# The last feed-forward block cut into groups of 4, 6, 6 and 6 chunks instead of 6, 8 and 8

## The chip, the cores and the metric

The kernel runs on one core of a Trainium2 chip. TensorE (PE) multiplies matrices, VectorE (DVE), ScalarE (ACT) and GpSimd (POOL) work elementwise, and transfers are issued from the queues of SyncE (SP), ScalarE and GpSimd. The metric is the device time of one execution in microseconds (us), as the median of several runs. Before the change it is 2786.47 us (3 runs, 2783.3 to 2787.67).

## The reference

Two trunk layers run over 512 latent tokens and 256 context tokens of width 1024. Each layer is half a SwiGLU feed-forward block, a mixer, and another half feed-forward block, so there are four feed-forward blocks, numbered f = 0 to 3 in the kernel. The last block, f = 3, runs over the 512 latent tokens alone, since the context is not part of the output.

```python
def swiglu(h, w1, w3, w2):
    return (jax.nn.silu(h @ w1) * (h @ w3)) @ w2

def _half_ffn(h, g, m, k, w1, w3, w2):
    y = swiglu(_modulate(h, g, m, k), w1, w3, w2)
    return h + (0.5 * m[:, :, 3 * k + 2] * y).astype(h.dtype)
```

`w1` and `w3` are 1024 x 2816, `w2` is 2816 x 1024. All arrays are float32.

## The kernel before, in words

Features lie on the 128 partitions and tokens on the free axis. The 2816 hidden features are 22 chunks of 128. A chunk needs two up products, one with `w1` (the gate) and one with `w3`; the two together are called a pair. A feed-forward block is cut into groups of chunks (`GROUPS`, L56). For each group the kernel first makes the hidden chunks (the pairs) and then one down pass: for each of the 8 output chunks j it multiplies the group's hidden chunks by their part of `w2` in PSUM and adds the result to the residual `x` (L2210). So each group costs one pass of 8 additions to `x`, and the matmuls of all the down passes together do not depend on the grouping.

Every float32 matrix product is made of three matmuls, because each operand is split into a rounded high part and the rest: weights times `hi`, weights times `lo`, and the weights' rest times `hi`. ACT makes the high part of a weight tile (L1362, L1427), DVE the rest by a subtraction (L2014, L2086). Weight tiles land in two buffers, `raw0` and `raw1`; the next transfer into a buffer starts when DVE has made the rest of the tile before (L569).

There are two kinds of pairs. A plain pair (first group of each block, `g == 0`) is 2 x 8 x 3 = 48 matmuls over all tokens, 512 columns each in the last block. A pair of seven products (all other groups; function `seven_products`, L791) splits both the weights and the tokens in halves and makes a 2 x 2 block product from seven products instead of eight (a Strassen-Winograd form): 7 x 4 x 3 = 84 matmuls over half of the tokens, 256 columns each in the last block. It needs sums of weight blocks. These are made ahead of time by accumulating transfers that GpSimd issues (`weight_sums`, L2902), in units of up to three pairs: seven transfers in four dependent steps, from HBM to HBM. A pair loads four tiles: two of sums into `raw` (L599), and `a11` and `a2` straight from the weights (L582, L588). It also needs sums of the tokens, made once for each block from the normalised activations: `sums(f, k)` for k = 0 to 3 on DVE (six instructions, L2062 to L2067), then `sum_hi` on ACT (L1399) and `sums_lo` on DVE (L2073). In a first group of six chunks all four are made behind the plain pairs 2 to 5. In a first group of four chunks, as in blocks 0 to 2, k = 0 and 1 are made behind pairs 2 and 3, and k = 2 and 3 in the down pass, at j = 1 and 3 (L1572, L2351, L2353).

The engines work their own programs in order and meet at semaphores. Around the change these orders matter. On ACT in a down pass, the high part of the tile for j + 2 comes first and then what `also(j)` holds. On DVE in a down pass, it is the addition to `x` of output j, then the rest of the tile for j + 2, then `also(j)`. In a pair of seven products, DVE makes the rests of `S1` and `A11` of the next pair before that of `A12` of this pair:

```python
                if not last:
                    weight_lo(f, g, i + 1, "S1")
                    weight_lo(f, g, i + 1, "A11")
                weight_lo(f, g, i, "A12")
```

The sixth product of pair i (on `A12`, L822) therefore waits for the sums of pair i + 1 to have landed. On GpSimd's queue the order is by hand (from L2978): the sums of the squares for a norm (`add_squares`) and the weight sums of the groups take turns. The sums of group 1 of the last block stand ahead of `add_squares(4)`, those of group 2 behind `add_squares(5)`, which ends just as the last block's first matmuls start.

Of the kernel before, what the change touches and what calls it, by code (L numbers as in the profile page):

```python
# [52 lines left out]


AB_IN_T, AB_OUT_T, CD_IN_T, CD_OUT_T = 24, 8, 20, 8
GROUPS = ((4, 6, 6, 6),) * 3 + ((6, 8, 8),)  # L56
HC = 6
BASE = {}
_t = 0
for _name, _n in (("ffn0", 2 * FC + KC * len(GROUPS[0])), ("ab_in", AB_IN_T), ("ab_out", AB_OUT_T),  # L60
                  ("ffn1", 2 * FC + KC * len(GROUPS[1])), ("ffn2", 2 * FC + KC * len(GROUPS[2])),
# [6 lines left out]
def first_chunk(f, g):  # L68
    return sum(GROUPS[f][:g])

# [12 lines left out]

NSEVEN = FC - GROUPS[0][0]

# [122 lines left out]
def build(nc, dr):  # L208
    ctx = ExitStack()
    with ctx:  # L210
# [1137 lines left out]
        def _(act):  # L1348
# [192 lines left out]
            def ffn(f, look, n_sq, ns, ns_sq):  # L1541
                n = NORM_OF[f]
                for g, size in enumerate(GROUPS[f]):
                    b, d, last = up_tile(f, g), down_tile(f, g), g == len(GROUPS[f]) - 1
                    for i in range(size):
                        ch, nk = first_chunk(f, g) + i, size if i == size - 1 else KC
                        if seven(f, g):
                            seven_act(f, g, i)
                            continue
                        if f and ch == 0:  # L1550
                            act.wait_ge(u_gate, 2 * LATE_UP.index(n) + 2)
                            act.activation(hidden_bufs(f)[0][:, 0, 0:ns], hfu[:, 0:ns], ACT.Copy).then_inc(h_hi, 1)
                            if f < 3:
                                act.wait_ge(h_ready, f * FC + 1)
                                load_scb(scb)
                                for q in range(2):
                                    load_mod(MODS[f][0] + q, mraw)
                            continue
                        plain_pair(f, ch, i, b + 2 * i, nk, ns)
                        if f == 0 and ch == 0:  # L1560
                            act.wait_ge(xn_ready, 8)
                            for q in range(2):
                                load_mod(q, mraw)
                        if 0 < f < 3 and ch == 1:
                            take_scb(f + 2, scb)
                        next_mods(f, ("up", ch))
                        if ch >= 2:
                            sum_hi(f, ch - 2)

                    def also(j):  # L1570

                        if f < 3 and g == 0 and j in (1, 3):  # L1572
                            sum_hi(f, 2 + j // 2)
                        if g == 0 and j == 5:
                            first_sum_hi(f)
                        if not last and j >= KC - 2:
                            for name in (("A11",), ("S1", "S2"))[j - KC + 2]:
                                weight_hi(f, g + 1, 0, name)
                        if j and not last:
                            next_mods(f, ("down", g, j - 1))  # L1580
                        if (f, g, j) == (2, 2, 3):
                            act.wait_ge(dl_set, 1)
                            act.activation(coef[:, 1, :], coef[:, 0, :], ACT.Exp, scale=-1.0).then_inc(coef_exp, 1)
                            act.wait_ge(dl_set, 3)
                            act.activation(dl[:, 2:4], dl[:, 0:2], ACT.Exp).then_inc(coef_exp, 1)

                    if last:
                        down(d, look, size, n_sq, ns_sq, also)
                    else:
                        down(d, 0, size, None, ns, also)  # L1590
# [411 lines left out]
        def _(dve):  # L2002
# [311 lines left out]
            def ffn(f, look, segs, nn=None):  # L2314
                n, ns = NORM_OF[f], segs[-1][1]
                for g, size in enumerate(GROUPS[f]):
                    b, d, last = up_tile(f, g), down_tile(f, g), g == len(GROUPS[f]) - 1
                    for i in range(size):
                        ch, nk = first_chunk(f, g) + i, size if i == size - 1 else KC

                        def ahead():
                            if f == 0 and ch < 2:
                                gate_dots(2 * ch)
                            if f < 3:
                                dot_mods(f, ("up", ch))

                        def behind():
                            if f == 0 and ch < 2:
                                gate_dots(2 * ch + 1)
                            if ch >= 2:  # L2330
                                sums(f, ch - 2)
                                sums_lo(f, ch - 2)

                        if seven(f, g):
                            seven_dve(f, g, i)
                        elif f and ch == 0:
                            bh, bl = hidden_bufs(f)
                            dve.wait_ge(h_hi, plain_chunk(f, 0) + 1)
                            dve.tensor_tensor(bl[:, 0, 0:ns], hfu[:, 0:ns], bh[:, 0, 0:ns].bitcast(F32), ALU.subtract
                                              ).then_inc(h_ready, 1)  # L2340
                        else:
                            plain_pair(f, ch, i, b + 2 * i, nk, ns, ahead, behind)
                    if f == 1 and g == 0:
                        late_gate(2)
                    if last and nn is not None:
                        prep(nn)

                    def also(j):

                        if g == 0:  # L2350
                            if f < 3 and j in (1, 3):  # L2351
                                sums(f, 2 + j // 2)
                            if f < 3 and j in (2, 4):  # L2353
                                sums_lo(f, 1 + j // 2)
                            if j == 5:
                                first_sum_lo(f)
                        if not last and j == KC - 2:
                            for name in ("A11", "S1", "S2"):
                                weight_lo(f, g + 1, 0, name)
                        if (f, g, j) == (2, 2, 2):  # L2360
                            cd_consts()
                        if (f, g, j) == (2, 2, 5):
                            cd_coefs()
                        if last or j < KC - 1:
                            dot_mods(f, ("down", g, j))

                    if last:
                        down(d, look, size, n, segs, nn, also)
                    else:
                        down(d, 0, size, n, segs, None, also)  # L2370
# [520 lines left out]
        def _(pool):  # L2891
# [10 lines left out]
            def weight_sums(f, g):  # L2902

                r, row = SEVEN_ROUNDS.index((f, g)), 2 * (f * FC + first_chunk(f, g))
                for i, n in sum_units(f, g):
                    base = 16 * SUM_DMAS * SUM_AT_UNIT[f, g, i]
                    tile = dr["w13"][row + 2 * i:row + 2 * (i + n)].rearrange("(i q) p c -> q p i c", q=2)
                    to = dr["sums"][r][:, i:i + n]
                    S = [to[:, :, q, :] for q in range(4)]
                    pool.wait_ge(sum_landed, base)  # L2910
                    pool.dma_start(S[0], tile[1][:, :, 0:512]).then_inc(sum_landed, 16)
                    pool.dma_start(S[1], tile[0][:, :, 0:512]).then_inc(sum_landed, 16)
                    pool.dma_start(to[:, :, 2:4, :].rearrange("p i b c -> p i (b c)"), tile[0]).then_inc(sum_landed, 16)
                    pool.wait_ge(sum_landed, base + 16 * 3)
                    pool.dma_start(S[0], tile[1][:, :, 512:D], accum_op=ALU.add).then_inc(sum_landed, 16)
                    pool.dma_start(S[2], tile[1][:, :, 0:512], accum_op=ALU.add).then_inc(sum_landed, 16)
                    pool.wait_ge(sum_landed, base + 16 * 5)
                    pool.dma_start(S[1], S[0], accum_op=ALU.add).then_inc(sum_landed, 16)
                    pool.wait_ge(sum_landed, base + 16 * 6)
                    pool.dma_start(S[3], S[1], accum_op=ALU.add).then_inc(sum_landed, 16)  # L2920
# [71 lines left out]
            add_squares(4, T)  # L2992
            cd_pool()
            add_squares(5, NLAT)
            weight_sums(3, 2)


def host_arrays(a):
# [110 lines left out]
```

## Time and profile before

| | us |
|---|---|
| median of 3 runs | 2786.47 |
| the profiled execution | 2784.83 |
| its span, first to last instruction | 2783.1 |
| TensorE busy | 2675.1 (96%) |
| VectorE busy | 2056.2 (74%) |
| ScalarE busy | 1176.3 (42%) |
| GpSimd busy | 390.2 (14%) |
| the last block's first down pass starts | 2486.9 |
| TensorE's last matmul ends | 2779.9 |

TensorE's busy share counts the modelled time of matmuls that overlap, so it says that the engine is rarely idle, and not at which rate it works. For the rate one takes a stretch without gaps and divides it by the number of matmuls in it. Times within the execution are counted from the span's start. "Landing" is the time from the issue of a transfer to its end. In the names of operands a buffer's number is left out: `a` is `a11` or `a2`, `wh` and `wl` are the high parts and rests of `raw`.

### The profile page before, as it was taken

The numbers are of one execution on the slowest core, as the hardware profiler recorded it, in microseconds if no ns is written. First come the engines' busy times: TensorE is split into PE (matmuls) and PEld (weight loads), VectorE is DVE, ScalarE is ACT, GpSimd is POOL, SyncE is SP. The second block draws the span as 40 slices with busy tenths as digits, with TensorE's granted clock in tenths as the row PEclk, the third lists the DMA queues.
The fourth block names the chain that finished last, engine by engine and source line by source line (L and its number), as shares of the span: only waits on it lengthen the run. The fifth ranks groups of instructions, "written<-read, shape, count | busy, mean of one in ns | idle before, by whom it ended". The sixth has DMA issues, their size and how long they took to land.

```text
span 2783.1 us, 40131 instructions
## 1 busy us (share of the span) xinstructions
PE 2675.1 (96%) x15624; PEld 2512.6 (90%) x15624; DVE 2056.2 (74%) x3184; ACT 1176.3 (42%) x1860; POOL 390.2 (14%) x312
## 2 busy tenths in 40 slices
PE   5999999999988999999999999999999989999999
PEld 5999999998976899999999999999997775788898
DVE  7887878774558587878777877787878667666674
ACT  3233333346447644332323523242436866533342
POOL 3111111110012521111111211100022410211000
PEclk8999999999999999999999999999999999999999
DMA  9888989621120047889897589874522110378453
GB/s 347 209 228 248 274 252 267 169 67 54 59 62 1 1 143 203 245 224 281 229 274 212 137 221 258 248 214 131 165 69 83 61 46 1 114 201 235 145 165 125
DMA packets 161691, 464.13 MB, mean 167 GB/s; under 512 B 13281, under 2 KB 14433, under 8 KB 160609
## 3 DMA queue, kind: packets, MB, share of 16 engines
q1 hardware_dynamic: 87200, 247.65, 26.3%
q0 software_dynamic: 56448, 146.81, 24.3%
q10 hardware_dynamic: 17856, 67.12, 6.8%
q8 instruction: 125, 2.05, 0.3%
q14 instruction: 62, 0.50, 0.0%
HBM read 459.43 MB, written 148.90 MB: 219 GB/s over the span
## 4 chain that ended last, share of the span: by engine, by line
PE 78%; DVE 11%; DMA 5%; ACT 3%; issue 3%; POOL 0%; ACTq 0%; SPq 0%; DVEq 0%; POOLq 0%
PE banks L698 11%; PE banks L702 11%; PE banks L700 11%; PE banks L786 9%; PE banks L788 9%; PE banks L787 9%; DMA raw<-sums 4%; PE banks L705 3%; PE banks L709 3%; PE banks L707 3%; DVE banks L2019 1%; DVE tmp L2292 1%; PE banks L1233 1%; DVE wl L2086 1%; DVE wl L2014 1%
## 5 line engine op out<-in xcount | busy, mean ns | idle before, releaser
L1362 ACT ACTIVATE wh<-raw 128x1024 fp32r<-128x1024 f32 (+2 forms) x194 | 181.8, 937 | 611.8 <-PE banks L702 458.7
L2019 DVE SCALAR_TENSOR_TENSOR banks<-mraw,scb 128x1024 f32<-128x1024 f32 x240 | 304.9, 1270 | 11.6 <-DMA mraw<-in_wmn 7.9
L2014 DVE TENSOR_TENSOR wl<-raw,wh 128x1024 fp32r<-128x1024 f32 (+2 forms) x216 | 234.3, 1085 | 95.5 <-ACT wh L1362 93.2
L1427 ACT ACTIVATE wh<-raw 128x512 fp32r<-128x512 f32 (+1 forms) x210 | 161.6, 774 | 326.6 <-DMA raw<-sums 156.7
L698 PE MATMUL banks<-hh,wh 128*128 128x384 f32 x1056 | 270.4, 337 | 9.3 <-DVE wl L2014 9.0
L786 PE MATMUL banks<-xh,wh 128*128 128x384 f32 (+1 forms) x796 | 258.0, 324 | 12.8 <-DVE wl L2086 12.7
L702 PE MATMUL banks<-hh,wl 128*128 128x384 f32 x1056 | 269.9, 336 | 0.0
L700 PE MATMUL banks<-hl,wh 128*128 128x384 f32 x1056 | 269.7, 336 | 0.0
L788 PE MATMUL banks<-xh,wl 128*128 128x384 f32 (+1 forms) x796 | 256.6, 322 | 0.0
L787 PE MATMUL banks<-xl,wh 128*128 128x384 f32 (+1 forms) x796 | 256.5, 322 | 0.0
L698 PE MATMUL banks<-xh,wh 128*128 128x384 f32 x880 | 230.7, 343 | 21.4 <-DVE xl L2284 12.0
L700 PE MATMUL banks<-xl,wh 128*128 128x384 f32 x880 | 225.2, 336 | 0.0
L702 PE MATMUL banks<-xh,wl 128*128 128x384 f32 x880 | 224.9, 336 | 0.0
L2086 DVE TENSOR_TENSOR wl<-raw,wh 128x512 fp32r<-128x512 f32 (+1 forms) x210 | 180.9, 866 | 43.6 <-ACT wh L1427 43.5
L698 PEld LDWEIGHTS banks<-hh,wh 128*128 128x128 f32 x1056 | 191.5, 189 | 11.5 <-DVE wl L2014 11.2
L702 PEld LDWEIGHTS banks<-hh,wl 128*128 128x128 f32 x1056 | 192.3, 189 | 0.0
L700 PEld LDWEIGHTS banks<-hl,wh 128*128 128x128 f32 x1056 | 192.2, 189 | 0.0
L698 PEld LDWEIGHTS banks<-xh,wh 128*128 128x128 f32 x880 | 158.4, 189 | 29.9 <-issue 16.0
L786 PE MATMUL banks<-th,wh 128*128 128x384 f32 (+1 forms) x560 | 180.5, 322 | 0.0
L787 PE MATMUL banks<-tl,wh 128*128 128x384 f32 (+1 forms) x560 | 180.5, 322 | 0.0
L788 PE MATMUL banks<-th,wl 128*128 128x384 f32 (+1 forms) x560 | 180.5, 322 | 0.0
L786 PEld LDWEIGHTS banks<-xh,wh 128*128 128x128 f32 x796 | 150.0, 188 | 16.3 <-DVE wl L2086 16.3
(427 smaller groups left out, 6225.5 us busy)
## 6 DMA issues: line engine op xcount, KB each, us to landing
raw<-sums SPq DMA_DIRECT2D x140, 512.0 KB, 6.0
sums<-in_w POOLq DMA_DIRECT2D x88, 768.0 KB, 8.5
mraw<-in_wmn ACTq DMA_DIRECT2D x120, 512.0 KB, 5.7
a<-in_w SPq DMA_DIRECT2D x70, 512.0 KB, 4.3
sums<-in_w POOLq DMA_DIRECT2D x22, 1536.0 KB, 8.8
sums<-sums POOLq DMA_DIRECT2D x44, 768.0 KB, 9.6
raw<-in_w SPq DMA_DIRECT2D x80, 384.0 KB, 4.3
raw<-in_w SPq DMA_DIRECT2D x52, 512.0 KB, 3.9
```

The costliest lines, as they stand in the source:

```text
L698: pe.matmul(bank(h), W, tokens(rh, h), start=(k == 0), stop=False)
L700: pe.matmul(bank(h), W, tokens(rl, h), start=False, stop=False)
L702: mm = pe.matmul(bank(h), L, tokens(rh, h), start=False, stop=(k == nk - 1))
L705: pe.matmul(G[slot][:, a:b], W, rh[:, k, a:b], start=(k == 0), stop=False)
L786: pe.matmul(thirds(bank), W, rh(k), start=(k == 0), stop=False)
L787: pe.matmul(thirds(bank), W, rl(k), start=False, stop=False)
L788: mm = pe.matmul(thirds(bank), L, rh(k), start=False, stop=(k == 3))
L1362: act.activation(wh[slot][:, 0:nk * P], raw[slot][:, 0:nk * P], ACT.Copy).then_inc(hi_done, 1)
L1427: act.activation(W_HI[slot_of(name, last)], W_SRC[name], ACT.Copy).then_inc(w_hi, 1)
L2014: dve.tensor_tensor(wl[slot][:, 0:nk * P], raw[slot][:, 0:nk * P], wh[slot][:, 0:nk * P].bitcast(F32), ALU.subtract).then_inc(lo_done, 1)
L2019: return dve.scalar_tensor_tensor(B67[:], tile, 1.0, scv[:, s, :], ALU.mult, ALU.mult, accum_out=out)
L2086: dve.tensor_tensor(W_LO[to], W_SRC[name], W_HI[to].bitcast(F32), ALU.subtract).then_inc(w_lo, 1)
```

## The change

`GROUPS[3]` becomes (4, 6, 6, 6), the same as for the other three blocks. All functions that go by `GROUPS` follow: the first group has four plain pairs (six before), the three others have 18 pairs of seven products (16 before), and there are four down passes of 4, 6, 6 and 6 chunks (three of 6, 8 and 8 before). Two of the four token sums move from the plain pairs into the first down pass, on ACT and on DVE. GpSimd makes weight sums for 6 pairs ahead of `add_squares(4)` (8 before) and for 12 pairs behind `add_squares(5)` (8 before).

```diff
-GROUPS = ((4, 6, 6, 6),) * 3 + ((6, 8, 8),)
+GROUPS = ((4, 6, 6, 6),) * 4
...
-                        if f < 3 and g == 0 and j in (1, 3):
+                        if g == 0 and j in (1, 3):
                             sum_hi(f, 2 + j // 2)
...
-                            if f < 3 and j in (1, 3):
+                            if j in (1, 3):
                                 sums(f, 2 + j // 2)
-                            if f < 3 and j in (2, 4):
+                            if j in (2, 4):
                                 sums_lo(f, 1 + j // 2)
...
-            weight_sums(3, 2)
+            for g in (2, 3):
+                weight_sums(3, g)
```

## Rows read from the trace of the kernel before

**Rows 1.** The page's first part: the span and TensorE's busy time.
```profile
span 2783.1 us, 40131 instructions
PE 2675.1 (96%) x15624; PEld 2512.6 (90%) x15624; DVE 2056.2 (74%) x3184; ACT 1176.3 (42%) x1860; POOL 390.2 (14%) x312
```

**Rows 2.** Busy times by stage, last block: stretch, length, engines (instructions), clock, transfers' share.
```profile
2465.10:2486.87 21.77, 21.77 (x97) 18.02 (x96) 14.67 (x22) 7.51 (x10) 2.25 (x3) 1.00 0.70 199
2486.87:2521.56 34.69, 33.24 (x145) 26.83 (x144) 18.62 (x26) 9.72 (x13) 4.68 (x4) 1.00 0.89 234
2521.56:2612.15 90.59, 83.21 (x674) 82.19 (x673) 65.91 (x111) 42.47 (x79) 6.99 (x8) 0.98 0.73 209
2612.15:2655.69 43.54, 43.54 (x194) 36.04 (x193) 17.29 (x20) 8.89 (x11) 0.00 (x0) 1.00 0.40 125
2655.69:2736.15 80.46, 80.46 (x673) 80.45 (x672) 64.75 (x109) 42.82 (x78) 0.00 (x0) 1.00 0.55 168
2736.15:2779.25 43.10, 43.10 (x193) 35.67 (x191) 15.50 (x17) 7.23 (x8) 0.00 (x0) 1.00 0.34 113
```

**Rows 3.** Waits of 2521 to 2612: who for whom, total us, times, longest.
```profile
ACT wh L1427 <- DMA raw<-sums: 20.9, 9, 5.6
...
PE banks L786 <- DVE wl L2086: 7.4, 5, 3.0
```

**Rows 4.** TensorE's timeline, second group, pairs 0, 1, 3: start, duration, instruction, idle before.
```profile
2531.87 0.38 PE L786 MATMUL banks<-xh,wh 128*128 128x256 f32 x1 [2.97 <-DVE wl L2086]
...
2533.59 0.42 PE L787 MATMUL banks<-tl,weh 128*128 128x256 f32 x1
...
2536.80 0.29 PE L787 MATMUL banks<-xl,wah 128*128 128x256 f32 x1
...
2543.88 0.39 PE L786 MATMUL banks<-xh,wh 128*128 128x256 f32 x1 [0.23 <-DVE wl L2086]
...
2567.31 0.39 PE L786 MATMUL banks<-xh,wh 128*128 128x256 f32 x1 [1.62 <-DVE wl L2086]
```

**Rows 5.** The chain that ended last, in the same pair: start, duration, what.
```profile
2522.47 6.76 DMA raw<-sums
...
2531.13 0.69 DVE wl L2086
```

**Rows 6.** GpSimd's timeline: starts of the last block's sum units, their last transfer, an earlier idle time.
```profile
2045.60 1.40 POOL L2896 COPY ssq<-sq 128x768 f32<-128x768 f32 x1 [206.06 <-ACT sq L1479]
...
2415.95 0.79 POOL L2911 DMA_DIRECT2D sums<-in_w  x1
...
2529.39 0.73 POOL L2911 DMA_DIRECT2D sums<-in_w  x1 [7.58 <-DMA sums<-sums]
...
2566.23 1.14 POOL L2920 DMA_DIRECT2D sums<-sums  x1 [7.29 <-DMA sums<-sums]
```

**Rows 7.** Issues, KB, median us to landing: 2490 to 2521, 2580 to 2736, whole span.
```profile
raw<-in_w SPq DMA_DIRECT2D x4, 384.0 KB, 6.1
...
raw<-sums SPq DMA_DIRECT2D x20, 512.0 KB, 3.6
...
raw<-in_w SPq DMA_DIRECT2D x24, 256.0 KB, 4.9
```

**Rows 8.** Timelines of VectorE and ScalarE at the first down pass's start.
```profile
2489.49 0.68 DVE L2062 TENSOR_TENSOR tmp<-xh,xl 128x512 f32<-128x512 f32 x1
...
2492.53 0.85 ACT L1399 ACTIVATE th<-tf 128x768 fp32r<-128x768 f32 x1 [4.02 <-DVE tf L2067]
...
2494.28 0.75 DVE L2210 SCALAR_TENSOR_TENSOR x<-banks,modG,x 128x512 f32<-128x512 f32 x1
2494.94 0.95 DVE L2014 TENSOR_TENSOR wl<-raw,wh 128x768 fp32r<-128x768 f32 x1
```

**Rows 9.** Block 2's first down pass (4 chunks, 768 tokens): as a stage, and TensorE's wait.
```profile
1633.80:1672.30 38.50, 35.56 (x194) 34.80 (x194) 33.83 (x55) 11.49 (x15) 4.94 (x4) 0.96 0.85 216
...
PE banks L698 <- DVE wl L2014: 2.9, 1, 2.9
```

## What the change should do to the time

> **What bounds the kernel now.** I read the page's first part first: TensorE is busy for 2675 of 2783 us [rows 1], so the time is TensorE's work plus its gaps. Then the stages of the last block [rows 2], which the change alone touches. In order they are two of the plain pairs, the first down pass (6 chunks), eight pairs of seven products, a down pass (8), eight more pairs, and the last down pass (8). The two halves do the same kind of work and don't take the same time: eight pairs take 90.6 us in the second group and 80.5 us in the third. Without gaps a 512-column matmul takes 43.54 / 192 = 0.227 us and a 256-column one 80.46 / 672 = 0.1197 us. At these rates the first down pass should take 144 x 0.227 = 32.7 us; it took 34.7, so it lost 2.0, and the second group lost 90.59 - 80.46 = 10.1.
>
> What differs is GpSimd. While it moves weight sums (from 2415.95 to the last transfer issued at 2566.23, landed near 2574 [rows 6]) the transfer engines are busy for 0.73 to 0.89 of the time, and for 0.34 to 0.55 after it [rows 2]. The waits name the link: ScalarE waits 20.9 us for tiles of sums to land, and TensorE 7.4 us, in five gaps, for a weight's rest [rows 3]. The chain shows one such gap [rows 5]: the tile lands 6.76 us after its issue, and ScalarE and VectorE need 2.6 us more until the rest for the sixth product begins (L2086 at 2531.13), because VectorE has the next pair's two rests ahead of it. In the third group a tile of sums lands in 3.6 us [rows 7], and TensorE has no gap. So the last block is bound by TensorE when GpSimd moves nothing, and by the landing of weights when it does.
>
> The first gap is 2.97 us. After it the matmuls start 0.12 us apart, and from 2533.4 to 2536.8 0.213 us apart: 15 matmuls at the 1.2 GHz level [rows 4], 15 x 0.093 = 1.4 us more. The granted clock of the stage is 0.98 where the others have 1.00 [rows 2]. The four shorter gaps of that group, 0.23 to 1.62 us [rows 4], have no such stretch behind them.
>
> **The change part by part.** Sums are against the profiled execution (2784.83 us, span 2783.1); the median is 1.64 us above it, and I add the same difference to the median.
>
> 1. TensorE's work. Two plain pairs go, 21.8 us, and two pairs of seven products come, 2 x 80.46 / 8 = 20.1 us [rows 2]. The down matmuls stay 22 x 8 x 3 = 528. Sum: -1.65 us. This is all that the change can gain by itself.
> The Trainium skill ("TensorE: Matmul & The Clock Gate", section "Wait — 56ns, not 53.3ns?") has a matmul of N columns start every N / 2.4 GHz + 2.5 ns. By that a plain pair is 10.4 us and a pair of seven 9.2 us, and the two would save 2.4 us. The trace is 5 to 10% slower at both widths and decides.
>
> 2. The first down pass with 4 chunks. I count from its start, D, to the sixth product of the next pair. Now this is 2531.87 - 2486.87 = 45.0 us, of which TensorE works 32.7 + 60 x 0.12 = 39.9: lost 5.1. With 4 chunks it works 21.8 + 7.2 = 29.0. What else must happen in this time is the order of VectorE and ScalarE: the last token sum of the plain pairs stands ahead of the tile for j = 2. With 6 chunks VectorE works on it from 2489.49, ScalarE makes its high part at 2492.53, and only then come the addition to x and the rest of the tile (2494.94 to 2495.9, D + 9.0) [rows 8], when the first two outputs took 8.2 us. With 4 chunks the tiles are a third narrower, so this comes at about D + 8.4, and TensorE is through with its two outputs at D + 5.9: a gap of 2.5 us. Block 2 has this pass at 768 tokens and shows that gap: 2.9 us, granted clock 0.96, 38.5 us for 192 x 0.173 = 33.3 us of matmuls, lost 5.2 [rows 9]. With 512 tokens the matmuls give a third less cover and VectorE's work does not shrink as much. Then two token sums follow at j = 1 and 3, of some 3.0 us on VectorE each (2489.49 to 2492.5 [rows 8]), with the tiles for j = 4 and 6 behind them on both engines: rests done at about D + 14.6 and D + 22. The narrow tile's landing of 4.9 us [rows 7] fits in beside this. The sums for the next pair are issued at D + 22, land 7 us later (6.76 in rows 5), and their second rest is ready 1.8 us after that, at D + 30.8; from there to the sixth product it is 9.4 us, as now (2522.45 to 2531.87). Together 40.2, lost 11.2, so +6.1 us. Bounds: as much lost as in block 2 and the 3.0 us gap of the pair after it, 8.2, so +3.1; or the tiles come at 9.2 us for two throughout, as they did in the present pass (ScalarE at 2502.21 and 2511.38), so lost 16, +11. I take +6.1, since the orders are those of the code.
>
> 3. The rest of the second group. From the sixth product on it lost 80.28 - 73.3 = 7.0 us (four gaps, and the stretch at 1.2 GHz). The group is now six pairs, of which the last has no next pair to wait for; the stalls were in pairs 0 to 4, and these remain. 0, with 1 us either way.
>
> 4. GpSimd's queue. It now moves 12 pairs of sums from 2416 on, in four units of three. A unit took (2529.39 - 2415.95) / 2 = 56.7 us [rows 6], so it ends at about 2643 and not at 2574. That is 69 us more under traffic. Nobody waits for the sums as such: the third unit lands near 2586, the last group starts near 2699. Ahead of `add_squares(4)` one unit of two pairs falls away; GpSimd idles for 206 us there [rows 6], TensorE has no gap then, so 0.
>
> 5. The second down pass, now 6 chunks under traffic. The tiles of 384 KB land in 6.1 us [rows 7]; with 0.85 + 0.96 us for the two halves the cycle of two tiles is 8.0 to 9.2 us against TensorE's 8.2, and it starts with two tiles in hand. +0.3, between 0 and +2.
>
> 6. The third group, first pair. Now it follows a pass of 6 chunks under traffic as the second group's did. The second rest would be ready about when the down pass ends, the sixth product 9.4 us later, TensorE's work before it 7.2: a gap of 2.2 us, and perhaps the slow stretch. I take +3.2, between 0 and 4.4 (3.0 + 1.4, what the second group paid).
>
> 7. Pairs 1 to 3 of the third group, from about 2610 to the end of the traffic. Without the first pair the second group lost 10.1 - 4.4 = 5.7 us in four pairs, 1.4 each (the gap and the restart): +4.2 us, between 0.7 (the smallest gap three times) and 6.5 (the largest four times).
>
> Sum: -1.65 + 6.1 + 0 + 0 + 0.3 + 3.2 + 4.2 = +12.15 us. Span 2795.3, execution 2797.0, median 2798.6 us. The lower ends give +1, the upper ones +24; they would not all meet.
>
> **The rivals.**
> Small: the traffic is spread thinner. In its last 69 us tiles land soon enough, and parts 5 to 7 give 1.5 us, with part 2 near its low end: +3 us, 2789.5. For it: the second pair's gap was only 0.23 us. Against it: the landing is what the five gaps of rows 3 have in common.
> Large: the first pass runs at 9.2 us for two tiles, the second pass loses 2 us, and the third group's stalls are as large as the largest: +20 us, 2806. For it: the present pass had this cycle twice.
> Clock: the Trainium skill (same page, section "HAM oscillation — how this bites in real kernels") tells of kernels in which each wait for a transfer puts TensorE back to half rate. Here that would be the 1.4 us stretch behind each of the about eight gaps that remain or come, in place of one or two: +8 us on the forecast, 2807. Only the gap of 2.97 us has such a stretch [rows 3, 4]; I give it little.
> Faster: the stalls of the second group depend on how a tile's landing meets the transfers of the sums. The group starts some 25 us earlier, in another unit. Were the tiles to land there within 7.2 - 2.6 = 4.6 us, the point from which it decides, its 10.1 us would go, and with a first pass at its low bound and nothing in the third group the sum is -1.65 - 10.1 + 3.1 = -8.6 us, 2778. Against it: all of the traffic's rows in this block lie above that point (6.1 and 6.76 us), and no unit differs from the others.
>
> **How the numbers follow.** Forecast 0.76, small 0.10, large 0.09, clock 0.03, faster 0.02. A difference of 0.2%, 5.6 us, is about the least that a measurement of this kernel can tell from no change. Forecast, large and clock lie above it: slower 0.88; small is within: same 0.10; faster 0.02. The range is 2791 to 2806, from +4.5 to +19.5: it leaves out most of the small and the clock case, and takes in the large one.
>
> **What would show it.** Right: GpSimd's last sum transfer near 2635 to 2643; a gap of 2 to 3 us on TensorE at the third output of the first down pass and smaller ones at the fifth and seventh, with VectorE's rest (L2014) as the releaser; a gap ahead of the sixth product in pairs 0 to 4 of the second and 0 to 3 of the third group; the last group at 10.06 us a pair without gaps; all before 2416 as it was. Wrong: if the second group has no gaps, part 3; if the third group runs at 10.06 us a pair while GpSimd's transfers go on, parts 6 and 7 and with them the link from traffic to stalls; if the last group too has gaps or the units take 70 us, the effect is larger than forecast.

## The result and the profile after

The changed kernel takes 2797.07 us (median of 5 runs, 2794.2 to 2803.6) against 2786.47 us before: a ratio of 1.0041, 95% interval 1.0029 to 1.0054. In a second series beside other kernels it was 2799.89 us against 2787.81, ratio 1.0048 (1.0028 to 1.0068). It is slower by 10 to 12 us, where +12.1 was forecast. Its profiled execution took 2796.72 us, with a span of 2794.9.

Gaps are given below from start to start of TensorE's matmuls; the idle time in a row is some 0.15 us shorter. These are the stages of the last block after the change, in the columns of [rows 2]: the first down pass (4 chunks), the second group (6 pairs of seven products), its down pass, the third group, its down pass, the fourth group, the last down pass.

```profile
2467.28:2494.75 27.47, 23.00 (x98) 17.71 (x97) 23.32 (x39) 8.61 (x13) 3.50 (x4) 1.00 0.86 256
2494.75:2570.30 75.55, 65.45 (x505) 64.43 (x504) 49.96 (x83) 33.03 (x60) 8.45 (x8) 0.93 0.90 240
2570.30:2602.97 32.67, 32.67 (x146) 27.05 (x145) 14.95 (x20) 7.39 (x10) 3.98 (x4) 1.00 0.86 226
2602.97:2665.92 62.95, 61.11 (x506) 60.50 (x504) 48.71 (x81) 32.03 (x58) 5.71 (x5) 1.00 0.87 235
2665.92:2698.59 32.67, 32.67 (x147) 27.04 (x146) 14.94 (x20) 7.39 (x10) 0.00 (x0) 1.00 0.42 130
2698.59:2758.93 60.34, 60.34 (x506) 60.34 (x505) 48.53 (x81) 31.80 (x58) 0.00 (x0) 1.00 0.54 167
2758.93:2791.14 32.21, 32.21 (x145) 26.66 (x143) 13.14 (x17) 5.71 (x7) 0.00 (x0) 1.00 0.37 121
```

The fourth group is the yardstick: 60.34 us for six pairs, TensorE busy throughout, transfers at 0.54, nothing on GpSimd. Where GpSimd issues transfers, their share is 0.86 to 0.90, and the same six pairs take 75.55 and 62.95 us. The four down chunks take 27.47 us for 96 x 0.227 = 21.8 us of matmuls. The second group also has stretches at the 1.2 GHz level, two of them, and its granted clock is 0.93.

TensorE's timeline shows the gaps themselves (start, duration, instruction, idle before it and who ended that), first in the down pass, then ahead of two sixth products:

```profile
2475.66 0.50 PE L705 MATMUL banks<-hh,wh 128*128 128x512 f32 x1 [2.35 <-DVE wl L2014]
...
2481.96 0.50 PE L705 MATMUL banks<-hh,wh 128*128 128x512 f32 x1 [0.57 <-DVE wl L2014]
...
2489.13 0.50 PE L705 MATMUL banks<-hh,wh 128*128 128x512 f32 x1 [1.41 <-DVE wl L2014]
...
2506.84 0.58 PE L786 MATMUL banks<-xh,wh 128*128 128x256 f32 x1 [4.13 <-DVE wl L2086]
...
2555.80 0.39 PE L786 MATMUL banks<-xh,wh 128*128 128x256 f32 x1 [3.64 <-DVE wl L2086]
```

The first three are the third, fifth and seventh output of the first down pass, each waiting for the rest of its weight tile on VectorE. The other two are the sixth products of pairs 0 and 4 of the second group. The chain that ended last at the start of this pass (start, duration, what) shows why: the order of [rows 8] stands ahead of that tile again, with narrower tiles.

```profile
2472.51 0.85 ACT th L1399
2473.39 0.96 DVE tl L2073
2474.35 0.66 DVE x L2210
```

GpSimd's timeline gives the length of the traffic. The first transfer of each unit is L2911, the last L2920:

```profile
2418.13 0.82 POOL L2911 DMA_DIRECT2D sums<-in_w  x1
...
2590.38 0.79 POOL L2911 DMA_DIRECT2D sums<-in_w  x1 [9.14 <-DMA sums<-sums]
...
2647.94 1.24 POOL L2920 DMA_DIRECT2D sums<-sums  x1 [10.64 <-DMA sums<-sums]
```

Three units took 172.3 us, 57.4 each. The fourth's last transfer is issued at 2647.9 and takes 9.0 us to land, so the sums end near 2657. [rows 6] had the last one issued at 2566.2: 82 us more of traffic.

Below I compare lengths of the last block alone, from its first matmul (L770) to the end of its last. Before it is 362.2 us (2417.7 to 2779.9), after it 371.9 (2419.9 to 2791.8): +9.7. The block's start is no measure of the change. In four profiled executions of kernels whose code is the same up to there but for one unit of sums (before, twice the changed kernel, and the experiment with traffic alone) it began between 2417.7 and 2432.4, since the pairs of seven in blocks 0 to 2 also stall, and not alike in each execution: TensorE waits 5.3, 2.9, 7.5 and 4.3 us for weights' rests (L2086) there in these four.

### The profile page after: what moved, and what is told of

Read it like the earlier page. It is cut to its first block, busy times and chain, and to the rows that moved or that the text cites. A ratio compares the mean times of both kernels' runs of the same rounds, so it can differ in the third digit from the quotient of the medians.

```text
span 2794.9 us, 40381 instructions
## 1 busy us (share of the span) xinstructions
PE 2678.7 (96%) x15696; PEld 2518.0 (90%) x15696; DVE 2071.2 (74%) x3220; ACT 1182.5 (42%) x1880; POOL 389.7 (14%) x312
## 3 DMA queue, kind: packets, MB, share of 16 engines
q1 hardware_dynamic: 89184, 249.22, 26.4%
## 4 chain that ended last, share of the span: by engine, by line
PE 76%; DVE 12%; DMA 5%; ACT 3%; issue 3%; POOL 0%; ACTq 0%; SPq 0%; DVEq 0%; POOLq 0%
PE banks L698 10%; PE banks L700 10%; PE banks L702 10%; PE banks L786 10%; PE banks L788 10%; PE banks L787 10%; DMA raw<-sums 4%; PE banks L705 3%; PE banks L709 3%; PE banks L707 3%; DVE banks L2019 1%; DVE wl L2086 1%; DVE tmp L2292 1%; PE banks L1233 1%; DVE wl L2014 1%
## 5 line engine op out<-in xcount | busy, mean ns | idle before, releaser
L2019 DVE SCALAR_TENSOR_TENSOR banks<-mraw,scb 128x1024 f32<-128x1024 f32 x240 | 304.6, 1269 | 15.5 <-DMA mraw<-in_wmn 11.8
L2014 DVE TENSOR_TENSOR wl<-raw,wh 128x768 fp32r<-128x768 f32 (+2 forms) x220 | 230.5, 1048 | 91.7 <-ACT wh L1362 89.9
L698 PE MATMUL banks<-hh,wh 128*128 128x384 f32 x1056 | 270.0, 336 | 10.2 <-DVE wl L2014 10.1
L786 PE MATMUL banks<-xh,wh 128*128 128x384 f32 (+1 forms) x816 | 264.9, 325 | 14.9 <-DVE wl L2086 14.8
L788 PE MATMUL banks<-xh,wl 128*128 128x384 f32 (+1 forms) x816 | 263.1, 322 | 0.0
L787 PE MATMUL banks<-xl,wh 128*128 128x384 f32 (+1 forms) x816 | 263.0, 322 | 0.0
L2086 DVE TENSOR_TENSOR wl<-raw,wh 128x512 fp32r<-128x512 f32 (+1 forms) x216 | 185.9, 865 | 56.5 <-ACT wh L1427 56.1
L698 PEld LDWEIGHTS banks<-hh,wh 128*128 128x128 f32 x1056 | 191.0, 189 | 12.5 <-DVE wl L2014 12.1
```

The lines of the kernel that those rows point to most:

```text
L698: pe.matmul(bank(h), W, tokens(rh, h), start=(k == 0), stop=False)
L786: pe.matmul(thirds(bank), W, rh(k), start=(k == 0), stop=False)
L787: pe.matmul(thirds(bank), W, rl(k), start=False, stop=False)
L788: mm = pe.matmul(thirds(bank), L, rh(k), start=False, stop=(k == 3))
L2014: dve.tensor_tensor(wl[slot][:, 0:nk * P], raw[slot][:, 0:nk * P], wh[slot][:, 0:nk * P].bitcast(F32), ALU.subtract).then_inc(lo_done, 1)
L2019: return dve.scalar_tensor_tensor(B67[:], tile, 1.0, scv[:, s, :], ALU.mult, ALU.mult, accum_out=out)
```

## The experiments

Theory: the changed kernel loses what was forecast in two ways, by stalls on tiles that land late beside GpSimd's traffic, and by the order of VectorE and ScalarE in the short first down pass. Rival: the traffic is not the cause, the cut into more and smaller pieces is. The first four ran beside each other, against a median of 2785.62 us of the kernel before (35 runs). The two with the last token sum moved ran against 2787.59 us, the others against 2787.81.

### Traffic taken out of the last block, groups 4, 6, 6, 6

```diff
-            weight_sums(3, 1)
+            for g in (1, 2, 3):
+                weight_sums(3, g)
             add_squares(4, T)
...
             add_squares(5, NLAT)
-            for g in (2, 3):
-                weight_sums(3, g)
```

> The changed kernel (groups of 4, 6, 6, 6), but GpSimd makes the weight sums of the last block's groups 2 and 3 ahead of add_squares(4), in its idle 244 us there, so that it moves nothing during the last block. Theory (part of the loss is stalls from GpSimd's traffic, part is the order of VectorE and ScalarE in the first down pass): no gaps in the pairs of seven products (10.3 + 4.3 + 2.6 us go), the gap of 2.5 us at the third output and the smaller ones at the fifth and seventh stay, lost from the pass's start to the sixth product 5.7 us where it is 10.6 now. Against the kernel before: -1.65 - 12.15 + 5.7 = -8.1 us, 2778. Rival (the extra down pass and the pairs themselves cost it, not the traffic): 2797 as the changed kernel.

Measured: 2782.11 us, ratio 0.9985 (0.9973 to 0.9997). The block takes 354.0 us, 8.2 less than before, as expected to 0.1. The first down pass and the second and third group:

```profile
2474.62:2502.08 27.46, 23.03 (x97) 17.70 (x96) 24.46 (x41) 9.66 (x15) 0.00 (x0) 1.00 0.37 116
2502.08:2562.42 60.34, 60.34 (x505) 60.34 (x504) 48.56 (x82) 31.70 (x58) 0.00 (x0) 1.00 0.55 172
2595.09:2655.43 60.34, 60.34 (x506) 60.34 (x505) 48.49 (x81) 31.86 (x58) 0.00 (x0) 1.00 0.53 166
```

Both groups run at the yardstick's 60.34 us. The down pass takes 27.46 us, the same as with traffic: what it loses there is not the landing of tiles. The whole kernel gained about 4 us (3.5 by the medians) and not 8. Part of the price is in block 2, where the sums now run beside the third and fourth group (87.96 and 89.83 us; 87.64 each without stalls, so 2.5 us). The rest was not traced to a place; the starts of the block spread by more than that.

### The same with groups 6, 8, 8

```diff
-            weight_sums(3, 1)
+            for g in (1, 2):
+                weight_sums(3, g)
             add_squares(4, T)
...
             add_squares(5, NLAT)
-            weight_sums(3, 2)
```

> The kernel before (groups of 6, 8, 8), with the same move: the weight sums of the last block's group 2 ahead of add_squares(4). Theory: of the 12.15 us that the first down pass and the second group lose, all go but the gap of 0.9 us behind the last token sum: -11 us, 2775. Then the grouping alone costs 3 us without traffic (first experiment less this one), and 10.6 with it. Rival (traffic is not what stalls the pairs): 2786.5, no change.

Measured: 2779.08 us, ratio 0.9976 (0.9961 to 0.9991), and a block of 351.1 us, 11.1 less than before. First down pass and second group:

```profile
2491.96:2525.68 33.72, 32.97 (x145) 26.95 (x144) 19.69 (x27) 9.80 (x13) 0.00 (x0) 1.00 0.42 125
2525.68:2606.13 80.45, 80.45 (x673) 80.44 (x672) 64.96 (x109) 42.71 (x78) 0.00 (x0) 1.00 0.55 173
```

So of the +9.7 us, the grouping itself is 354.02 - 351.07 = 3.0 us, and the rest is that traffic costs 17.9 us in the last block with the new groups (371.9 - 354.0) and 11.1 with the old ones.

### Traffic alone, groups 6, 8, 8

```diff
             weight_sums(3, 2)
+            row, n0 = 2 * (3 * FC + first_chunk(3, 2)), len(SUM_AT_UNIT)
+            for q, (i, n) in enumerate(((0, 3), (3, 1))):
...
+                to = dr["sums"][0][:, i:i + n]
```

(Not shown here are the transfers themselves, the seven of L2911 to L2920 once more for a unit of three pairs and one of a single pair, into rows that are no longer read.)

> The kernel before (6, 8, 8) with traffic alone: after its last unit GpSimd moves four more pairs' sums (a unit of three and one of one) into rows of the sums that are long used up, so that transfers go on from 2574 to about 2650. Nothing else is changed. Theory: pairs 5 and 6 of the second group get gaps like pairs 1 to 4 (1.4 us each), the second down pass with tiles of 8 chunks has cover and loses nothing, the third group starts after the traffic: +1 to +4 us, 2789. Rival (what the change cost in its third group is from the grouping): 2786.5, no change.

Measured: 2792.93 us, ratio 1.0021 (1.0007 to 1.0036), block 370.5 us: +8.4 in the profiled execution, about +6 by the ratio and +7.3 by the medians. The direction is the theory's, the size is two to three times the +2.5 us of the forecast. Second group and its down pass:

```profile
2529.43:2629.27 99.84, 86.28 (x674) 84.98 (x673) 66.10 (x110) 41.67 (x78) 13.23 (x14) 0.95 0.89 243
2629.27:2672.86 43.59, 43.59 (x194) 35.99 (x193) 17.35 (x20) 9.89 (x12) 6.23 (x8) 1.00 0.76 197
```

The group takes 99.8 us where it took 90.6 [rows 2]: pairs 5 and 6, which had no gap before, now have one of 2.8 us each, twice the 1.4 us that I had put on a pair, and a stretch at the 1.2 GHz level behind each (1.5 and 1.2 us). These two add up to 8.4 us; the other changes cancel. Pair 2, ahead of the extra traffic, had 3.2 us where it had 1.4 before, and pair 3 none where it had 1.8, so single pairs are not comparable between executions. The down pass with 8 chunks loses nothing beside the same traffic. GpSimd's last transfer is issued 241.5 us after its first, where the changed kernel has 229.8 us and the kernel before 150.3. With traffic of such a length the old groups pay 11.1 + 8.3 = 19.4 us for it, and the new ones 17.9 us (19.7 in a second execution, shown last). So in these executions the cost of the traffic goes with its length; the cut into more pieces adds nothing to it that they show.

### A12 ahead of the next pair's sums, traffic kept

```diff
+                weight_lo(f, g, i, "A12")
                 if not last:
                     weight_lo(f, g, i + 1, "S1")
                     weight_lo(f, g, i + 1, "A11")
-                weight_lo(f, g, i, "A12")
```

(The same on ScalarE, and in the list that counts the steps.)

> The changed kernel with the traffic where it is, but ScalarE and VectorE make the halves of A12 of this pair ahead of S1 and A11 of the next pair, in all blocks. Theory (the sixth product waits only since VectorE has the next pair's sums ahead of it): the gaps ahead of the sixth product go, 4.3 + 2.3 + 3.8 us and 1.4 us for each slow stretch in the second group and 2.1 us in the third, less what comes back where sums land too late for the next pair's second product: -8 to -12 us against the changed kernel, 2785 to 2789. Rival (the stall is the cycle of the two buffers, and only moves to the next pair's second product): 2797.

Measured: 2786.48 us, ratio to before 1.0007 (0.9995 to 1.0019), so 10 to 13 us below the changed kernel, as expected, but not where it was expected. The last block takes 370.1 us, 1.8 less. The waits of TensorE from the second group to the end of the third down pass (who for whom, total us, times, longest) say where the stall went:

```profile
PE banks L786 <- DVE u L2138: 5.7, 4, 3.0
PE banks L705 <- DVE hl L2102: 2.6, 2, 2.3
PE banks L786 <- DVE wl L2086: 2.6, 4, 1.3
```

VectorE still stands at the next pair's `S1` until that has landed, and now it is its next step, the combination `u` (L2138), which the seventh product waits for. This stall is smaller: the second group takes 68.8 us and not 75.6. But the third down pass takes 36.8 us and not 32.7. Its first output waits 2.27 us for the low part of the last hidden chunk (`hl`, L2102), behind a tile of `w2` that took 7.43 us to land beside the last sums, and a stretch at the 1.2 GHz level follows that costs 1.7 us:

```profile
2662.72 0.66 PE L705 MATMUL banks<-hh,wh 128*128 128x512 f32 x1 [2.27 <-DVE hl L2102]
```

So in the last block the rival was nearly right: most of the stall came back in other places. In blocks 0 to 2, whose pairs are longer, it did not come back. TensorE waits 2.9 to 7.5 us there for weights' rests (L2086) in five profiled executions without this edit, and not at all in this one. These are two of block 0 and block 2 that took 90.13 and 89.50 us before:

```profile
305.98:393.62 87.64, 87.64 (x505) 87.64 (x505) 74.01 (x111) 35.33 (x58) 9.69 (x9) 1.00 0.88 245
1669.15:1756.79 87.64, 87.64 (x506) 87.64 (x505) 72.50 (x109) 35.83 (x59) 9.81 (x12) 1.00 0.90 265
```

The two profiled executions account for 4.9 us of the 10 to 13: 1.8 in the last block and 3.1 by an earlier start of it. Where the rest lies in the other executions is not shown.

### The token sums in the first down pass cut short, traffic taken out

```diff
                 a, b = tmp[2][:, 0:ns], tmp[3][:, 0:ns]
+                if f == 3 and k >= 2:
+                    chain(dve.tensor_tensor(thirds(s1[:, k, :]), half(a, 1), half(a, 0), ALU.subtract))
+                    dve.tensor_tensor(thirds(sf[:, 2, :]), half(b, 0), thirds(sf[:, 0, :]), ALU.subtract).then_inc(tf_set, 1)
+                    return
```

> As e1_after_early (4, 6, 6, 6, no transfers of GpSimd in the last block), but of the token sums k = 2 and 3 of the last block, which the change moved into the first down pass, VectorE makes two of the six instructions (the products on these sums are then made of stale numbers; nothing else is left out). Some 2 us less on VectorE at j = 1 and at j = 3. Theory (the gaps at the fifth and seventh output, 0.7 and 1.6 us, are VectorE's and ScalarE's order around these two sums; the 2.5 us at the third output belongs to the sum ahead of the pass): the pass loses 3.4 us where e1 lost 5.7, TensorE's gap at the third output stays. From the last block's first matmul to its last 2.3 us less than e1's 353.6. Rival (these gaps are the landing of small tiles): the same 353.6.

Measured: a block of 351.4 us, 2.6 less than in the first experiment (2783.00 us in all, ratio 0.9978, 0.9963 to 0.9993). The down pass and its one remaining gap:

```profile
2480.55:2505.39 24.84, 22.35 (x97) 17.87 (x96) 20.86 (x33) 9.89 (x15) 0.00 (x0) 1.00 0.42 128
...
2488.93 0.50 PE L705 MATMUL banks<-hh,wh 128*128 128x512 f32 x1 [2.35 <-DVE wl L2014]
```

The gaps at the fifth and seventh output are gone, the one at the third is as long as ever. So the four instructions left out of each of the two moved sums cost 2.6 us there. Of the other 3.1 us, 2.5 are the gap at the third output. Some 0.4 are at the end of the first output, where TensorE reaches the fourth hidden chunk before VectorE has made its low part (`hl`, L2055).

### Both remedies, with either grouping

The sums ahead of `add_squares(4)` (the edit of the first or second experiment) together with the order of the fourth, once with 6, 8, 8 and once with 4, 6, 6, 6:

> A version meant to be fast: the kernel before (6, 8, 8), the sums of group 2 of the last block ahead of add_squares(4), and the halves of A12 ahead of the next pair's sums in all blocks. Expected from e2 (-6.7 us) and from e3, whose blocks 0 to 2 ran their pairs of seven without gaps where before they lost 4 to 10 us: -11 to -15 us, 2771 to 2775, and the last block no faster than in e2. Rival (the blocks' stalls differ from run to run by other causes): 2779, as e2.

> The same with the changed kernel's groups (4, 6, 6, 6). The difference to the run before it is the grouping alone, without traffic and without the order that makes pairs wait for it. Theory: 1.65 us less of matmuls, 5.7 instead of 1.1 us lost in the first down pass: +3 us. Rival (without stalls the two more pairs of seven gain what they save): -1.65 us.

Measured: 2771.74 us with 6, 8, 8 (ratio 0.9951, 0.9935 to 0.9967; block 351.1 us) and 2774.78 us with 4, 6, 6, 6 (0.9958, 0.9944 to 0.9972; block 354.1 us). The difference is +3.0 us in the medians and in the blocks. Without stalls and with one order for both, the grouping alone costs 3 us. The blocks are as long as in the first two experiments, to 0.1 us, so what the order gained here lies before them: their profiled executions start the block 8.7 and 14.5 us earlier.

### The last token sum behind the tile of j = 2

```diff
-                        if ch >= 2:
+                        if 2 <= ch < size - 1:
                             sum_hi(f, ch - 2)
...
+                        if g == 0 and j == 0:
+                            sum_hi(f, size - 3)
```

(The same for `sums_lo` on VectorE. Everything else is as in the two kernels just shown.)

> v6 (6, 8, 8, no traffic in the last block, A12 first), and in all blocks the high part and the rest of the last token sum of the plain pairs are made in the down pass at j = 0, behind the tile for j = 2. Theory (the gap at the first down pass's third output is this sum standing ahead of the tile on VectorE and ScalarE): the gap of 3.0 us and the stretch at 1.2 GHz behind it (lost 4.8 us together) shrink to about 1 us in blocks 0 to 2, and the 0.9 us of the last block go: -9 to -12 us against v6, 2760 to 2763. Rival (the tile lands late, or the instructions of the sum itself are what fill VectorE): no more than -3 us.

> The same with groups of 4, 6, 6 and 6 in the last block. Theory: of the 5.7 us that its first down pass loses, about 2 go (the gap of 2.5 us shrinks to 0.5 to 0.8), the gaps around the two token sums in the pass stay: the last block takes 1.5 to 2 us more than that of v8 and not 3.0 more. Rival (without this gap the two more pairs of seven pay): 1 us less than v8.

Measured: 2763.66 us with 6, 8, 8 (ratio 0.9914, 0.9895 to 0.9934) and 2768.11 us with 4, 6, 6, 6 (0.9932, 0.9913 to 0.9951). Blocks 350.0 and 353.0 us. The first is the fastest kernel of this study, 24 us below the kernel before; the gain over the run without this edit is 8.1 us and not 9 to 12. The first down pass of block 0 takes 36.2 us where it took 38.4 in the kernel before. First down passes of the last block, 6 chunks and 4 chunks:

```profile
2478.68:2511.32 32.64, 32.64 (x145) 27.03 (x144) 19.78 (x27) 9.94 (x13) 0.00 (x0) 1.00 0.42 131
...
2455.66:2482.08 26.42, 22.95 (x97) 17.71 (x96) 24.34 (x41) 9.77 (x15) 0.00 (x0) 1.00 0.41 121
```

With 6 chunks the pass is now without a gap. With 4 it still loses 26.4 - 21.8 = 4.6 us: the gap at the third output shrank from 2.5 to 0.6 us as expected, but the one at the fifth grew from 0.7 to 1.6. VectorE is busy for 24.3 of 26.4 us; its two longest idle times are 0.77 us each, both waiting for ScalarE's high part of the tile for the fifth and the seventh output, which stands behind a token sum's high part. So what bounds the pass then is the work on VectorE and its order with ScalarE. The difference of the groupings stayed at 3.0 us in the blocks, where I had expected 1.5 to 2. In the medians it is 4.5 us.

### The changed kernel once more

> The changed kernel once more beside the others, for its interval: 2786 + 10 = 2796 us by the theory and by its first five runs.

Measured: 2799.89 us. Its profiled execution (span 2809.2, block 373.7 us) shows first down pass, second and third group:

```profile
2479.76:2510.03 30.27, 24.62 (x97) 18.88 (x96) 24.63 (x41) 9.88 (x15) 3.51 (x4) 0.94 0.80 244
2510.03:2573.05 63.02, 62.00 (x506) 60.69 (x505) 47.61 (x80) 30.77 (x56) 7.22 (x7) 1.00 0.96 270
2607.66:2680.21 72.55, 65.24 (x506) 64.63 (x505) 48.82 (x81) 31.87 (x58) 5.71 (x5) 0.93 0.77 216
...
2627.87 0.58 PE L786 MATMUL banks<-xh,wh 128*128 128x256 f32 x1 [2.81 <-DVE wl L2086]
...
2654.21 0.50 PE L786 MATMUL banks<-xh,wh 128*128 128x256 f32 x1 [3.34 <-DVE wl L2086]
```

Here the second group loses 2.7 us and the third 12.2; in the first profiled execution it was 15.2 and 2.6. The sum hardly differs, the places do. The two matmuls are the sixth products of pairs 1 and 3 of the third group, the 145th and the 313th of its matmuls.

## Why the prediction was right, and where it was right by luck

**TensorE's work (part 1).** Right. Six pairs at 60.34 us are 10.06 each, as before, and all down passes without a gap run at 0.227 us a matmul. The Trainium skill's spacing ("TensorE: Matmul & The Clock Gate", section "Wait — 56ns, not 53.3ns?") would have put them 5 to 9% closer; in no stretch without gaps here are they.

**The first down pass (part 2).** Right in mechanism and size: from the pass's start to the sixth product 2506.84 - 2467.28 = 39.6 us where 40.2 was forecast, +5.5 us against +6.1. The gap at the third output is 2.5 us as worked out, and the seventh's and fifth's are there. One reading in it does not follow from its rows: at 0.227 us a matmul TensorE is through with two outputs at D + 5.4 and not D + 5.9. It was D + 5.9 because of the 0.4 us wait for the fourth hidden chunk, which the prediction does not name, so that the gap came out at 2.5 and not 2.9 us is luck. The 40.2 us are counted along VectorE's times and do not hang on it. The experiment with the short sums shows two of its three gaps to be the moved sums, and the last pair of versions shows the third to be the sum ahead of the tile. What bounds the pass there is VectorE's work: with that sum moved the pass gained only 1.0 us. The pass lost the same with and without traffic in this execution (27.47 and 27.46 us); in the second one of the changed kernel it lost 2.8 us more.

**The rest of the second group (part 3).** Wrong in size: forecast +0, within 1. It lost 2570.30 - 2506.84 - 53.2 = 10.3 us where it had lost 7.0: +3.3. The step that failed is that pairs 0 to 4 stall after the change as before, at the same price. Behind the sixth product of pair 0 three pairs stalled (1, 3 and 4) and not four. But one gap there was 3.8 us (idle 3.64), longer than any before, and two stretches at the 1.2 GHz level, of 2.2 and 1.5 us, follow gaps where there had been one of 1.5. These stretches are 2.2 of the 3.3 us. In the second execution the same part lost less than 3 us.

**GpSimd's queue (part 4).** The sums last until about 2657 and not 2643: the first three units took 57.4 us each where 56.7 was forecast, and the fourth 66.5 to its last landing. Nobody waited for the sums. The unit of two pairs that fell away in block 2 should change nothing; the start of the last block spreads too much to tell.

**The second down pass (part 5).** Forecast +0.3, measured 0 in one execution and 1.95 in the other. There the wait (1.63 us, at the first output) is for the low part of the last hidden chunk (L2102) and not for the cycle of the two tiles, which the forecast names; a tile that took 7.96 us to land stands ahead of it on VectorE.

**The third group's first pair (part 6).** Wrong in both executions: forecast +3.2, measured no gap. The step that failed is that this pair would stall because it follows a pass of 6 chunks under traffic, as the second group's did. The prediction has the tile that the sixth product hangs on issued when the down pass ends and landing in 7 us. It was issued 1.3 us before that end in both executions (at 2601.68 and 2606.36) and landed in 4.5 and 5.6 us. So 4.6 us, which the prediction names as the point from which it decides, was not the point here: with 5.6 us the rest was done 0.4 us before TensorE needed it. In the second execution the first gap comes one pair later, behind a tile that took 7.3 us.

**Pairs 1 to 3 of the third group (part 7).** Forecast +4.2, measured 62.95 - 60.34 = 2.6, with gaps in pairs 2 and 4 (idle 1.09 and 0.73 us) and none in pairs 1 and 3. In the second execution it was 12.2 us, with gaps in pairs 1, 3 and 4 and two stretches at the 1.2 GHz level (2.4 and 1.4 us).

Together -1.65 + 5.5 + 3.3 + 0 + 0 + 2.6 = +9.75 us for the block, and it was +9.7. The spans of the two profiled executions differ by 11.8 us; the other 2 are that the block starts 2.2 us later, which lies within the spread of the starts. The forecast's sum was 2.4 us above. Parts 3 and 6 missed by 3.3 and 3.2 us in opposite directions. The four stages from the first down pass to the third group lost 5.7 + 15.2 + 0 + 2.6 = 23.5 us in the first execution and 8.5 + 2.7 + 1.95 + 12.2 = 25.3 in the second; the forecast had 25.9. It had their total right, and their places wrong. That two executions with stalls in other places have nearly the same total may be more than luck, but two are too few to show it, and why the landing differs from one to the other stays open. The traffic's price can be taken from the blocks: 17.9 and 19.7 us in the two executions with the new groups, against 11.1 with the old ones.

The rivals: the small case is refuted by the third group's 12.2 us in the second execution; in the first the third group alone (2.6 us) would not have told it from the forecast. The large one would have needed the 9.2 us cycle throughout, and the tiles for the fifth and seventh output came 6.3 and 7.2 us after the ones before (2475.66, 2481.96, 2489.13). For the rival on the clock: in the first execution the idle times of 4.13 and 3.64 us have a stretch at the 1.2 GHz level behind them and those up to 2.35 us have none. The two cost 3.7 us where one cost 1.5 before, so this took 2.2 of the 9.7 us; a stretch behind every gap did not come. The faster case came in neither time, but its mechanism is to be seen in the second execution: the second group lost 2.7 us where it had lost 10.1 before. The first pass and the third group took up what it gave. One reading of [rows 5] in the prediction is off: from the tile's landing (2529.23) it is 1.9 us until VectorE begins the rest for the sixth product and 2.6 until it is done; the sums use it rightly.

## What to carry to other kernels

Ask of a regrouping not only what the matmuls save but what each smaller piece still has to cover: here TensorE had 5.9 us of work in the short pass until its third output, whose tile was ready after 8.4 us, and without traffic this pass lost 4.6 us more than the one of 6 chunks (5.7 against 1.1), almost three times the 1.65 us that the two cheaper pairs gained. Background transfers belong where the foreground has cover to spare; the same sums stall pairs of 10 us more than those of 14.6 us, and moving them there brought the kernel before 6.5 us. And in an in-order queue the step that waits for a transfer should stand behind all that is already there: two such swaps of order and one move of the sums brought 24 us, and in the last block the grouping under study cost 3 us each time.

## What the runs showed of the hardware

A tile of sums of 512 KB landed in 3.5 to 3.7 us with nothing on GpSimd's queue and in 3.7 to 8.3 us beside its transfers, within the last block of the first execution of the changed kernel; one of 8.1 us was issued 2 us after a transfer of 1536 KB, which itself took 10.4 us. That they belong together was not tried. The moved traffic did not slow matmuls as such: groups in blocks 0 and 2 run at 87.64 us with a transfer share of 0.88 to 0.90. After idle times of TensorE of 2.97 us before the change and 4.13 and 3.64 us after it, 16 to 24 matmuls of 256 columns ran at the 1.2 GHz level, and the slow stretch began up to 1.5 us after the engine had resumed, not with the gap. The length of the idle time alone does not decide it. In the last block, 2.61, 2.81 and 3.34 us in the second execution of the changed kernel, 2.70 and 2.68 us with traffic alone and 2.27 us with `A12` first had a stretch behind them; 2.97 us with `A12` first, 3.04 us with traffic alone and 2.35 us in six executions had none. Earlier in the kernel, ahead of the last block, most executions show one near an idle time of 1.89 us. What decides it stays open here. Executions of one kernel spread over 2778 to 2797 us (35 runs), which is as much as the effects studied, so lengths of a stage within the execution told more than whole times.
